# Three groups of quarter products instead of one in each gated feed-forward stage

## The reference

```python
def swiglu(h, w_gate_up, w_down):
    a, b = jnp.split(h @ w_gate_up, 2, axis=-1)
    return (jax.nn.silu(a) * b) @ w_down

x = x + 0.5 * swiglu(rms_norm(x, ffn1_norm), ffn1_w_gate_up, ffn1_w_down)
...                                   # pooling, attention, gates
x = x + 0.5 * swiglu(rms_norm(x, ffn2_norm), ffn2_w_gate_up, ffn2_w_down)
```

## Time and profile before

| what | us |
|---|---|
| time, median of 3 runs (1427.32 to 1428.21) | 1427.74 |
| the profiled execution's own time | 1427.59 |
| its span, first to last instruction | 1425.7 |
| TensorE busy | 1420.4 |
| TensorE's weight loads busy | 1220.6 |
| VectorE busy | 1036.0 |
| ScalarE busy | 824.6 |
| GpSimd busy | 178.8 |

### The profile page before, as it was taken

How to read it: one execution, slowest core, us unless ns; L and a number is a source line. 1 busy time by engine, 2 the same in 40 slices (tenths; PEclk the granted TensorE clock), 3 DMA queues, 4 the chain that set the end, 5 groups by cost and what they waited for, 6 DMA issues and landing times.

```text
span 1425.7 us, 20628 instructions
## 1 busy us (share of the span) xinstructions
PE 1420.4 (100%) x7920; PEld 1220.6 (86%) x7920; DVE 1036.0 (73%) x1634; ACT 824.6 (58%) x1405; POOL 178.8 (13%) x243
## 2 busy tenths in 40 slices
PE   9999999999999999999999999999999999999999
PEld 8888888898888888888888898888888899888887
DVE  7866776676866768666676678766776867778776
ACT  6665556754655556565466745655557765455553
POOL 0200023000000002000050004000048300100000
PEclk9999999999999999999999999999999999999999
DMA  9786565354777448874564556786546435456651
GB/s 382 259 237 196 181 208 187 134 192 165 265 240 216 157 154 280 243 214 164 177 236 148 162 179 234 239 227 189 187 155 222 134 121 194 160 168 218 199 184 59
DMA packets 77137, 280.33 MB, mean 197 GB/s; under 512 B 8560, under 2 KB 8688, under 8 KB 76912
## 3 DMA queue, kind: packets, MB, share of 16 engines
q1 hardware_dynamic: 72144, 261.46, 53.2%
q0 software_dynamic: 4608, 16.78, 6.6%
q10 hardware_dynamic: 288, 0.79, 0.1%
HBM read 277.94 MB, written 1.05 MB: 196 GB/s over the span
## 4 chain that ended last, share of the span: by engine, by line
PE 100%; DVE 0%; issue 0%; POOL 0%; POOLq 0%
PE bank L672 26%; PE bank L679 13%; PE bank L626 9%; PE bank L627 9%; PE bank L628 9%; PE bank L693 4%; PE bank L698 4%; PE bank L694 4%; PE bank L656 3%; PE bank L663 3%; PE bank L657 3%; PE bank L831 2%; PE bank L832 2%; PE bank L835 2%; PE bank L929 1%; PE bank L646 1%
## 5 line engine op out<-in xcount | busy, mean ns | idle before, releaser
L1890 DVE TENSOR_TENSOR wlo<-raw,whi 128x1024 fp32r<-128x1024 f32 (+1 forms) x457 | 549.4, 1228 | 12.2 <-ACT whi L1292 12.2
L1292 ACT ACTIVATE whi<-raw 128x1024 fp32r<-128x1024 f32 (+1 forms) x457 | 465.8, 1048 | 11.7 <-PE bank L835 6.1
L672 PE MATMUL bank<-hx,whi 128*128 128x512 f32 x1600 | 391.1, 392 | 0.0
L672 PEld LDWEIGHTS bank<-hx,whi 128*128 128x128 f32 x1600 | 295.9, 188 | 61.4 <-issue 3.0
L679 PEld LDWEIGHTS bank<-hx,wlo 128*128 128x128 f32 x1600 | 208.6, 191 | 10.1
L626 PE MATMUL bank<-whi,hid 128*128 128x512 f32 x536 | 211.8, 395 | 0.0
L679 PE MATMUL bank<-hx,wlo 128*128 128x256 f32 x1600 | 211.7, 282 | 0.0
L627 PE MATMUL bank<-wlo,hid 128*128 128x512 f32 x536 | 209.8, 391 | 0.0
L628 PE MATMUL bank<-whi,hid 128*128 128x512 f32 x536 | 208.8, 390 | 0.0
L1321 ACT ACTIVATE hid<-prod 128x256 fp32r<-128x256 f32 x110 | 46.0, 418 | 167.9 <-DVE prod L2041 82.5
L628 PEld LDWEIGHTS bank<-whi,hid 128*128 128x128 f32 x536 | 100.7, 188 | 21.8
(11 more groups left out here) (297 smaller groups left out, 1934.6 us busy)
## 6 DMA issues: line engine op xcount, KB each, us to landing
raw<-w_dram SPq DMA_DIRECT2D x462, 512.0 KB, 4.4
gates<-w_dram POOLq DMA_DIRECT2D x32, 512.0 KB, 6.5
gates<-w_dram SPq DMA_DIRECT2D x16, 512.0 KB, 9.2
gain<-g_dram SPq DMA_DIRECT2D x7, 512.0 KB, 3.7
arena<-c_dram SPq DMA_DIRECT2D x2, 768.0 KB, 6.2
cst<-c_dram SPq DMA_DIRECT2D x1, 1056.0 KB, 5.7
out_dram<-x SPq DMA_DIRECT2D x4, 256.0 KB, 2.0
par<-p_dram SPq DMA_DIRECT2D x1, 867.0 KB, 7.4
```

Of the source, the lines that this page charges most:

```text
L672: e.matmul(b[:, :], hi_of(j)[:, k * P:k * P + P], hx[:, k * 2 * S:k * 2 * S + 2 * S], start=k == 0, stop=False, skip_group_check=True)
L1292: e.activation(hi_of(t), raw_of(t), ACT.Copy).then_inc(sem["w_hi"], 1)
L1890: e.tensor_tensor(lo_of(t), raw_of(t), hi_of(t).bitcast(F32), ALU.subtract).then_inc(sem["w_lo"], 1)
```

## The change

- `GROUPS` is (9, 13, 18): three groups of four blocks per gated stage, named a, b, c. Eight normal pairs are left (N2 to N8 and N17). The products are numbered anew; 1 and 2 share a bank, 7 and 4 share one.
- `ORDER` is one list of steps that every engine follows: `N5` is a normal pair, `d5` the accumulation of hidden tile 5, `3b` product 3 of group b, `T0b` the first set of transposes of group b. The order inside the first three blocks changes with it: `input_low` comes after block 3 and no longer after block 4, and ScalarE's `input_forms` comes ahead of the hidden tile of block 3.
- A second pair of form buffers, G1 and H1, lies in `arena`; group b uses it, a and c use G0 and H0. SP waits for the squares and for `ylo` before it loads into them.
- `TURNED` says after which step the hidden tiles of a group are formed.
- POOL issues its accumulating loads in the order of the steps, and prepares the next stage's rope tables after 6a's instead of ahead of all.
- Some semaphores are merged: the pool constants share one, the output stores share one, the halves of a first form share one.

```diff
-GROUPS = (18,)
-SLOTS = {4: ((0, 0),), 6: ((0, 1),), 8: ((0, 2),), 10: ((0, 3),), 12: ((0, 4),), 14: ((0, 5),), 16: ((0, 6),)}
+ORDER = """N2 N3 d0 1a N4 d1 3a 2a N5 d2 7a N6 d3 6a 5a N7 d4 4a N8 d5 3b 1b d6 T0a 7b d7 T1a 2b 6b d8 5b d9 4b 3c
+           d10 T0b 1c d11 T1b 7c d12 2c 6c d13 5c N17 4c d14 d15 T0c d16 T1c d17""".split()
+GROUPS = (9, 13, 18)
...
-FORMS = (("G", 0), (None, 0), ("H", 0), ("H", 1), ("H", 2), ("G", 1), ("H", 3))
+FORMS = {1: ("G", 0), 2: (None, 0), 3: ("H", 0), 7: ("H", 1), 6: ("H", 2), 5: ("G", 1), 4: ("H", 3)}
...
+def turned_hidden():
+
+    at, out = {word: n for n, word in enumerate(ORDER)}, {}
+    for i, (c, q) in CHUNK.items():
+        n = max(at[f"T{q // 2}{'abcde'[c]}"], at[f"d{i - 4}"])
+        out.setdefault(n, []).append(i)
+    return out
...
+                if kind == "T":
+                    claim((tag, "turn", i, k), "hidlo", self.HID0[st] + GROUPS[i] + 2 * k + 2)
+                if kind == "P" and k == 1:
+                    held[i, 1] = claim((tag, "s", i, 1), "sil", 2 * cc + 1, True)
+                if kind == "P" and k == 2:
+                    ring.append(held[i, 1])
+                if kind == "P" and k == 3:
+                    claim((tag, "s", i, 3), "tokv", cc + 1)
+                if kind == "P" and k == 7:
+                    held[i, 7] = claim((tag, "s", i, 7), "comb", 5 * cc + 5, True)
+                if kind == "P" and k in (5, 6):
+                    claim((tag, "s", i, k), "comb", 5 * cc + 7 - k)
+                if kind == "P" and k == 4:
+                    ring.append(held[i, 7])
...
-        form = {"G": gates[:, 0:2 * TW], "H": gates[:, 2 * TW:4 * TW]}
+        form = {"G0": gates[:, 0:2 * TW], "H0": gates[:, 2 * TW:4 * TW], "G1": arena[:, 0:2 * TW], "H1": arena[:, 2 * TW:4 * TW]}
...
+                    if c >= 2:
+                        E.wait_ge("w_lo", SI[T[f"{tag}s{c - 2}{last}{h}"]] + 1)
+                    elif c == 1:
+                        E.wait_ge("sq", 4 * STAGES.index(tag) + 3)
+                        E.wait_ge("sq_v", 1)
+                        if buf == "H":
+                            E.wait_ge("xf_lo", GATED.index(tag) + 1)
...
                        # ScalarE
+                        low(i, 1)
+                        if i == 3:
+                            input_forms()
                         E.wait_ge("mul", K.MULV[s, i])
                         hidden_hi(K.HID0[s] + i, prod[m % 2][:, :])
...
+                    if kind == "d":
+                        ahead(T[f"{tag}d{i}"])
+                        catch_up()
+                    if kind == "P":
+                        ahead(T[f"{tag}s{i}{n}0"])
+                        catch_up()
+                        ahead(T[f"{tag}s{i}{n}1"])
+                        due.append((i, n))
+                    for h_ in TURNED.get(at, ()):
+                        catch_up()
+                        if h_ == NF - 1:
+                            hi_upto(T[f"{tag}d{h_}"])
+                        turned(h_)
...
                        # VectorE
+                        if i == 2:
+                            input_sum(0)
+                            input_sum(1)
+                            input_forms()
+                        if i == 3:
+                            input_low()
...
                # POOL
+                for _, kind, c, n in steps():
+                    if kind != "P":
+                        continue
+                    if n not in (2, 4, 5):
+                        add_form(tag, c, n)
+                    if c == 0 and n == 4:
+                        if nt == "M":
+                            prepare2(s + 1)
+                        elif nt in ("L0", "L1"):
+                            prepare1(s + 1, int(nt[1]))
```

More of the change, by code:

```diff
@@ L130, in gated @@
         plan.extend((f"{tag}p{k}", m * 512, True) for k, m in a_group(512))
-        for i in range(2, NF - 1):
-            if i not in CHUNK:
+        for _, kind, i, n in steps():
+            if kind == "N":
                 plan.extend([(f"{tag}a{i}", TW, True), (f"{tag}b{i}", TW, True)])
[L134 to L137, removed]
+            if kind == "d":
+                plan.append((f"{tag}d{i}", TW, True))
+            if kind == "P":
+                plan.extend((f"{tag}s{i}{n}{h}", TW, True) for h in range(2))
         plan.extend((f"{tag}d{i}", TW, True) for i in range(NF - LAST, NF))
@@ L284, in chunk_no, with form_no @@
         return GATED.index(tag) * len(GROUPS) + c
+    def form_no(self, tag, c):
+        same = [i for i in range(len(GROUPS)) if set_no(i) == set_no(c)]
+        return GATED.index(tag) * len(same) + same.index(c)
     def banks(self):
@@ L298, in claim, with gated @@
             return b
[L300 to L314, removed]
+        def gated(tag, st):
+            held = {}
+            for _, kind, i, k in steps():
+                cc = self.chunk_no(tag, i)
+                if kind == "N":
+                    claim((tag, "a", i), "sum", self.SUMV[st, i] + 1)
+                    if i == 2:
+                        claim((tag, "ft", 0), "hidlo", self.HID0[st] + 2)
+                    claim((tag, "b", i), "sum", self.SUMV[st, i] + 2)
+                if kind == "T":
[12 more added lines that the diff above has]
+                    ring.append(held[i, 7])
         for st, tag in enumerate(STAGES):
@@ L616, in sp_program @@
                     E.wait_ge("x", 28 + 2 * a + h + 1)
[L617 to L620, removed]
+                    e.dma_start(out[a * P:a * P + P, h * 512:h * 512 + 512], xq(a, h)).then_inc(sem["st"], 16)
+            E.wait_ge("st", 64)
         def pe_program(E):
@@ L856, in from_tokens @@
                     return ins
[L858 to L863, removed]
+                for _, kind, i, n in steps():
+                    if kind == "T":
+                        turn_chunk(s, i, n)
+                    elif kind == "P":
+                        product(s, i, n)
+                    elif kind == "d":
+                        accum(s, i)
                     else:
@@ L2016, in gated, with catch_up @@
                 due = []
[L2017 to L2025 removed]
+                def catch_up():
+                    while due:
+                        chunk(*due.pop(0))
+                for at, kind, i, n in steps():
+                    if kind == "N":
                         ja, jb = T[f"{tag}a{i}"], T[f"{tag}b{i}"]
```

238 lines of the change are left out of this document (108 added, 130 removed).

## The result

The changed kernel takes 1480.87 us (median of 4 runs, 1475.92 to 1484.97) against 1427.74 for the kernel before on the same chip: a ratio of 1.0371, 95% interval 1.0354 to 1.0388. It is 53 us slower. A fourth run of the kernel before took 2011.42 us, far off its other three, and is left out. The prediction of 1430.0 was wrong, and so was its range, which ended at 1441. The profiled execution took 1479.05 us.

What follows compares the result with a forecast made beforehand. It took TensorE, busy 1420.4 of 1425.7 us, as the bound. Per stage -4.40 + 1.3 + 3.45 + 0.2 = +0.55, over four stages +2.2, gave 1430.0 by the median; the 8-in-10 range was 1417 to 1441.

Steps and rivals of the forecast that it cites:

- TensorE saves 4.40 us a stage: Per gated stage eight pairs go, 14 products and four turns come: 4.40 us less, 17.6 over four stages.
- a sign against it: Listed under what would show it wrong: busy TensorE time not down by about 17.6 us.
- The wait after N3, 1.3 us: Low matmuls of N4b and d1 wait behind ylo on VectorE: 1.3 us per stage, bounds 0 to 2.3.
- The wait at 5b, 3.45 (1.1 to 6.3): Before 5b TensorE waits for T1a's bank, held by hidden tile 12 behind a late add: 3.45 us per stage.
- the landing of 7b's second add: In the chain to 5b, put 2.1 us later than a quiet pair's landing at 17.1 after N8's end.
- 9 + 5.3 us of engines from 8.5 on: DMA engine time for three adds and 3.5 loads around 7b's adds, counted from N8's end on TensorE.
- The small ones at 4b, 0.2: 4b waits for the third combining operation after 5b, 0.2 us beyond d9.
- In group a the hops have a pair between them: nothing: Hops between group a's products are 11 to 13.7 us apart, so no wait was priced.
- 7c to 6c: nothing: Tight hop, 8.2 us apart, with no hidden tile behind it whose bank the next product claims: no wait.
- DMA as a whole: no stall beyond the chain: Per stage 61 loads and 24 adds make 156 to 176 us in 178: no further stall, but no slack.
- C: Rival: each add pair between 7b and 4b lands as the worst row; 5b waits up to 6.3; 1441; chance 0.27.
- D: Rival: DMA bounds the stage, an add costing over 3.6 us of the engines; 1446 and up; chance 0.05.

Runs made afterwards that it cites:

- y3_two_late: Two groups of four blocks instead of the changed kernel's three, front mended, d7 ahead of 3b and d8 ahead of T0a: 1419.12 us, ratio 0.9945 to the kernel before.
- x1_front: The changed kernel with the low split of N4b ahead of the low part of the transformed input on VectorE: 1483.18 us, ratio 1.0396.
- x4_stream: The changed kernel with SP streaming all product tiles through raw buffers, without form buffers or adds: 1437.14 us, ratio 1.0067.
- x3_plain: The changed kernel with POOL's 96 accumulating loads as plain loads, same bytes and order: 1439.18 us, ratio 1.0083.
- y2_three: The changed kernel's three groups with ylo behind the splits of N4b and d1, d8 ahead of T1a, 5c ahead of d13: 1485.48 us, ratio 1.0399.
- x6_half: The changed kernel with accumulating loads taking only the first 512 of each tile's 1024 columns: 1440.59 us, ratio 1.0093.
- x2_bank: The changed kernel with d8 moved ahead of T1a, so that 5b's bank is free in time: 1485.66 us, ratio 1.0398.

## Why the prediction was wrong

Point by point, by its own steps:

- **TensorE saves 4.40 us a stage: right.** One group more without new waits brought 8.5 us (y3_two_late), where two groups more were to bring 17.6. The busy time did not fall by 17.6, and the prediction had named that as a sign against it. But other things hide the saving, 1423.4 - (1420.4 - 17.6) = 20.6 us: 11.8 of lower clock (below), and 0.26 of busy time for each of 31 gaps, 8.1.
- **The wait after N3, 1.3 us: right in place.** Shown is 0.92 to 0.94 at N4b and nothing at d1; mended (x1_front) it comes back as 1.18 at d1, so the queue on VectorE was as I had it.
- **The wait at 5b, 3.45 (1.1 to 6.3): right in place and mechanism, short in size.** The bank of T1a, hidden tile 12 and ScalarE standing at 4b's add are all in the trace: the wait ends with the subtraction of the hidden tile. It measured 2.45 in the row shown and 3.0 to 3.3 in the other stages. But 6b and d8 just ahead already wait for the same chain, which I had not seen: 11.8 + 6.5 + 3.1 = 21.4 in four stages, 5.4 each where I had 3.45. The term that was too small is the landing of 7b's second add. I put it 2.1 us later than quiet, at 9.2 after its issue; it took 12.2, 10.7, 11.6 and 10.8 in the four stages, 3.6 to 5.1 later than quiet. The working had pointed there: 9 + 5.3 us of engines from 8.5 on end at 22.8, which is 5.7 behind the quiet 17.1, and the 2.1 doesn't follow from it. (The first landing stands as 14.4 where 8.8 + 5.2 is 14.0; the second one decides, so nothing hangs on it.) x4_stream shows the lower end: 0.99, where I had 1.1.
- **The small ones at 4b, 0.2: right in size,** 0.26 in two of the stages, 0.31 in x4_stream.
- **"In group a the hops have a pair between them: nothing": this failed.** It put the hops of 11 to 13.7 us at nothing by their length alone, without a working. In the 11 us from 7a to 6a an add landed 8.4 us after its issue, and a high split, six splits of VectorE and a combining operation came on top before N7's bank was free. N7 and 5a lost 10.5 + 1.4 us, and the clock behind the gap as well. The worst landings were known, and I carried them through at 5b alone.
- **"7c to 6c: nothing": right for 6c and 7c, but 4c and T0c were missed,** 1.9 and up to 0.9 a stage, also without any chain (x4_stream, T0c in three stages): the combining operation on VectorE stands in a queue of splits. I had worked out the 18 splits between N8 and 3c and drawn no wait from them.
- **"DMA as a whole: no stall beyond the chain": right in its totals.** Adds cost what I took (2.88 us of the engines, against 2.7 to 3.5), and the stages' DMA share of 0.80 to 0.86 is 155 to 172 us of engines, where I had 156 to 176. But the engines are full just when an add is to land. Two stretches of L0f1 with two adds of group b in flight:

```profile
114.00:116.00 2.00, 2.00 (x13) 1.66 (x12) 1.98 (x3) 2.00 (x4) 0.87 (x1) 1.00 1.03 258
...
118.00:120.00 2.00, 2.00 (x11) 1.65 (x10) 1.29 (x2) 0.00 (x0) 0.00 (x0) 1.00 1.02 231
```

  These adds, issued at 112.98 and 114.30, landed 9.6 and 12.2 us later, and ScalarE stood still from 118 on. The Trainium skill, "DMA: Bandwidth & Descriptors", "Queues, rings and completion order", has each engine take turns between its queues packet by packet; by it loads in flight always slow an add. The trace agrees, with landings of 9.6 and 12.2 us at a DMA share of 1.02 to 1.03 against 5.2 quiet, though earlier adds were in flight as well and no row parts the two.
- **The clock was no term at all.** The mean granted clock fell to 0.992, 0.008 x 1477 = 11.8 us. In the kernel before TensorE waited only twice, 1.0 and 1.1 us at the kernel's start, so its rows showed no price for a gap beyond the gap.

What the 53 us consist of, by the experiments: -17.6 for the matmuls, + 27.3 for the order without a chain (x4_stream), + 2.0 for the chain with plain loads (x3_plain against x4_stream), + 41.7 for the adding (the changed kernel against x3_plain). The last one holds the longer waits and nearly all of the clock's 11.8. These shares hold for this order of taking things out: with the adds kept, mending the order's own gaps gains nothing (y2_three).

Of the span's 51.5 us the trace gives: -17.6 for the matmuls, + 48.1 of gaps more than before, + 8.1 for 31 gaps beyond their brackets, + 11.8 of clock, 50.4 in all.

Of the rivals C, the chain of adds decides, was the right one, and mis-sized: it let the chain decide at one place (5b) and at full clock, and ended at 1441. D gave a time in the right direction (1446 and up) by a condition that did not come: an add cost 2.88 us of the engines and not over 3.6.

Open stays how the adding's 41.7 us divide between an add's own length and the loads that it holds up.

## What to carry to other kernels

A resource that works in a chain (here add, split, product, next add) is to be priced at each hop with its landing under load, not where the order looks tightest; if it is slower than the hops allow, mending the place of the gap only moves the gap. Where a change trades bounded work of the busiest engine for such a chain, do the smaller step first: two groups with other work between the products gained 8.5 us, three lost 53. And a gap in front of TensorE costs more than its length, so a sum that only adds gaps is a lower bound.

## What the runs showed of the hardware

- An accumulating load of 512 KB keeps the DMA engines 2.88 us, a plain one issued from the same queue 1.54; its issue on POOL takes 0.87 us against 0.53. Its quickest landing was 5.2 us and that of the plain one 3.5; the medians are 7.5 and 4.8, the longest 14.4 and 11.6. An add of half the bytes (x6_half) keeps the engines 1.65 us.
- TensorE's clock behind a gap. The pair N7 in three stages of the changed kernel, beside the row at 84.83 above (16 matmuls, the gap before them in brackets):

```profile
430.38 3.91 PE L716 MATMUL bank<-hx,whi 128*128 128x512 f32 x16 [1.63 <-issue]
...
623.25 5.44 PE L716 MATMUL bank<-hx,whi 128*128 128x512 f32 x16 [2.32 <-issue]
...
970.03 5.49 PE L716 MATMUL bank<-hx,whi 128*128 128x512 f32 x16 [2.95 <-issue]
```

  Behind 1.63 us they ran as ever, behind 2.32 and 2.95 they took 1.6 to 1.7 us more than 3.79, behind 3.55 they took 2.8 more. But it is not the gap's length alone. The same 16 matmuls took 3.89 us behind 2.40 in x1_front and 5.40 behind 2.14 in x2_bank. And at 6b of the changed kernel, behind 1.84 us at 127.58, the granted clock was 0.50 in the stretch 129 to 131, while behind the 1.84 us at 665.11 it was 1.00 up to 671, as it was behind 1.90 at 181.06. TensorE had been busy without a gap from 86 to 125 before the first of these. What makes the difference these rows don't show.
